# Twelve pairs of units in the second input projection as seven half-size products each

## The chip, the cores and the metric

One core of a Trainium2 chip runs one program. The metric is the device time of one execution in microseconds, the median of the runs. The engines are TensorE (PE, its weight loads PEld), VectorE (DVE), ScalarE (ACT), GpSimd (POOL) and SyncE (SP, which here only issues DMAs). Each takes its own instructions in order; semaphores tie them together.

## The reference

Two layers run one after the other on x of 1024 tokens by 1024 features, in float32. The first (attention, two recurrent mixers and a feed-forward part) is not touched. The second is:

```python
h = rmsnorm_2(x, norm_gain)
z = jnp.einsum('bsd,de->bse', h, w_in)               # 1024 -> 4864 columns
q, k, v, gate_a, u_in, v_in, gate_b, g_merge = jnp.split(z, IN_SPLITS, axis=-1)
...
attn = block_attention(q, k, v) * jax.nn.silu(gate_a)
y_a = jnp.einsum('bse,ed->bsd', attn, w_proj_attn)
u = jax.nn.gelu(u_in)
vv = layernorm(jax.nn.gelu(v_in), ln_v_gain, ln_v_bias)
vv = vv.reshape(B, S // CHUNK_2, CHUNK_2, N_GROUPS, GROUP_DIM)
v_mix = jnp.einsum('gij,bcjgd->bcigd', w_spatial, vv) + b_spatial.T[:, :, None]
gm = u * v_mix.reshape(B, S, GMLP_WIDTH) * jax.nn.silu(gate_b)
y_b = jnp.einsum('bse,ed->bsd', gm, w_proj_gmlp)
g = jax.nn.sigmoid(g_merge.reshape(B, S, N_BRANCHES, D_MODEL) + b_merge)
y = g[:, :, 0, :] * y_a + g[:, :, 1, :] * y_b
return x + jnp.einsum('bsd,de->bse', y, w_out)
```

## The kernel before, in words

Every large product is made of three: each operand is split into a high part (`h_hi`, `w_hi`, rounded to the matmul's type) and a low part (`h_lo`, `w_lo`, the rest), and hi x hi, lo x hi and hi x lo are added in PSUM. Activations are held transposed: features on the 128 partitions, tokens along the free axis, in eight row blocks. A **unit** is 128 columns of a weight matrix: for each half of 512 tokens eight row blocks by three matmuls of 128x512, 48 matmuls. Its result fills two of the four `gemm` banks. GpSimd splits a unit's weights (w_hi, then w_lo, 128x1024 each) as soon as the unit that used the same buffer two before is done.

The units of the second projection have kinds: `vi` (v_in), `ga` and `gb` (the gates), `u2` (u_in), `sga` and `sgb` (the two halves of g_merge). ScalarE evicts each with its function: gelu, silu or sigmoid.

The first block's gate and up projections already use another scheme, the item **mul**: two units are taken together, as a 2x2 block matrix of weights (column block, feature half) times one of activations (feature half, token half), by seven products of half size in place of eight (Strassen-Winograd's kind). A product has four row blocks by three matmuls, 12, in one bank. Five of the seven weights are sums of two blocks (`weight_sum`, GpSimd; `wsum`), each is rounded by ScalarE (`hi_of_quarter`) and its low part made by GpSimd (`weight_low`). Five of the activations' blocks are sums too, made once: three in own tiles (`cmb`), two in the place of blocks that nobody needs any more. After the products ScalarE copies three to `m1`, `m4` and `m3`, and VectorE adds them up in eight operations in `mul`, four of which (`final`) give a quarter of the result. The products of a pair come in the order `MUL = (0, 3, 1, 2, 4, 6, 5)`; the first takes bank 1, then 2, 3, 0, 1, 2, 3, so the fifth needs the first one's bank and its weight slot.

The function `schedule` writes one list of items, and every engine walks through it and emits its part of each item; so the list sets the order on each engine. After the attention (`a2...`) it has: `vi` 0 to 3 with their transposes (`viT`), `ga` 1, `ga` 2 with `ln` behind it, `ga` 3, `u2` 0 to 3, `gb` 0 followed by four `sp` items, `gb` 1 by four more, `gb` 2 and 3, `split4`, and then four rounds of `sga`, `sgb`, `ya`, `yb`.

- `ln` is the layer norm of vv. TensorE transposes w_spatial (`wsr` to `wsT`); VectorE copies half of wsT, sums vv, subtracts the mean; ScalarE squares (`lsq`); VectorE makes the reciprocal root and runs sixteen passes over vv (L2584 and L2586). The last signals `ln_done`.
- `sp` c is the spatial product of a chunk of 128 tokens, 16 matmuls of vv by wsT into one of four side banks, which rotate. TensorE waits for `ln_done` ahead of `sp` 0. VectorE evicts with the bias (L2612) and multiplies into uT (L2613).
- `split4` rounds aoT (gated attention) and uT to hi and lo for `ya` and `yb`, the output projections of the branches (24 matmuls a unit); these are multiplied by the sigmoid tiles and added to yT. `splity` rounds yT for the last projection, `wo2`.

Of the kernel before, what the change touches and what calls it, by code (L numbers as in the profile page):

```python
# [70 lines left out]
def weight_units():  # L71
# [48 lines left out]
    add("w_in_2", 8, 0, [(O2_V, 128)], [("v2", 0)])  # L120
    add("w_in_2", 8, 0, [(O2_GA, 128)], [("ga", 0)])
    for o, kind in ((O2_VI, "vi"), (O2_GA, "ga"), (O2_U, "u2"), (O2_GB, "gb")):
        for j in range(kind == "ga", 4):
            add("w_in_2", 8, 0, [(o + 128 * j, 128)], [(kind, j)])
    for j in range(0, 8, 2):
        for s in range(2):
            add("w_in_2", 8, 0, [(O2_M + 128 * (j + s), 128)], [("sga", j + s)])
        for s in range(2):
            add("w_in_2", 8, 0, [(O2_M + 1024 + 128 * (j + s), 128)], [("sgb", j + s)])
# [2520 lines left out]
```

## Time and profile before

| | |
|---|---|
| runs before, median (lowest to highest) | 2293.89 us (2293.43 to 2296.59) |
| profiled execution, its own time | 2298.19 us |
| its span, first to last instruction | 2296.4 us |
| mean granted TensorE clock | 0.976 |
| TensorE / VectorE / ScalarE / GpSimd busy | 92% / 53% / 38% / 39% |

The page's busy shares are means over very different stages. Times of rows are microseconds from the span's start. Matmuls overlap in the profile: each is shown with 0.39 us, but they start 0.23 us apart.

### The profile page before, as it was taken

How to read it: one execution, taken by the hardware profiler on the slowest of the kernel's cores; microseconds unless marked ns; L12 is line 12 of the kernel's file. 1: busy time of each engine (PE TensorE's matmuls, PEld its weight loads, DVE VectorE, ACT ScalarE, POOL GpSimd, SP SyncE). 2: the span in 40 equal slices, each digit the busy share in tenths (PEclk: the TensorE clock that was granted, in tenths of full speed). 3: DMA queues.
4: the chain of work that ended last, by engine and by line, in shares of the span. 5: the costliest groups of instructions: out<-in, count | busy, mean ns of one | idle time of the engine just before them, and what ended most of it. 6: DMA issues, size and time to landing. Idle time of an engine off the chain costs nothing. (4 is left out here: it accounts for less than half of the span.)

```text
span 2296.4 us, 29464 instructions
## 1 busy us (share of the span) xinstructions
PE 2122.5 (92%) x10819; PEld 1781.0 (78%) x10819; DVE 1228.5 (53%) x1811; ACT 863.4 (38%) x1562; POOL 889.4 (39%) x612
## 2 busy tenths in 40 slices
PE   6999988878998999999999968879999999999997
PEld 6788877768787788888877757768887888888886
DVE  4443503866547734444489897679995235110232
ACT  4332216555224443434444544238774122000112
POOL 1232331331335688888732642220000333333334
PEclk9999999989999999999999989999999999999999
DMA  4111310021222122222274534200001111111131
GB/s 153 41 46 46 83 55 19 19 48 36 85 71 84 43 58 68 72 70 68 78 243 140 186 101 143 93 28 1 1 2 33 47 47 39 53 46 47 54 119 74
DMA packets 181824, 157.44 MB, mean 69 GB/s; under 512 B 27588, under 2 KB 147120, under 8 KB 181552
## 3 DMA queue, kind: packets, MB, share of 16 engines
q1 hardware_dynamic: 163904, 119.05, 17.5%
q10 hardware_dynamic: 17776, 36.51, 4.3%
q8 instruction: 87, 1.43, 0.3%
q14 instruction: 57, 0.47, 0.1%
HBM read 134.03 MB, written 21.50 MB: 68 GB/s over the span
## 5 line engine op out<-in xcount | busy, mean ns | idle before, releaser
L1123 POOL TENSOR_SCALAR w_hi<-w_raw 128x1024 fp32r<-128x1024 f32 x91 | 105.9, 1163 | 940.9 <-issue 893.6
L1235 PE MATMUL gemm<-h_hi,w_hi 128*128 128x512 f32 x1072 | 423.6, 395 | 4.9 <-POOL h_lo L1152 4.9
L1237 PE MATMUL gemm<-h_hi,w_lo 128*128 128x512 f32 x1072 | 419.1, 391 | 0.0
L1236 PE MATMUL gemm<-h_lo,w_hi 128*128 128x512 f32 x1072 | 419.1, 391 | 0.0
L1235 PEld LDWEIGHTS gemm<-h_hi,w_hi 128*128 128x128 f32 x1072 | 202.6, 189 | 49.4 <-issue 8.7
L1237 PEld LDWEIGHTS gemm<-h_hi,w_lo 128*128 128x128 f32 x1072 | 202.3, 189 | 42.7
L1236 PEld LDWEIGHTS gemm<-h_lo,w_hi 128*128 128x128 f32 x1072 | 202.7, 189 | 40.8
L1126 POOL TENSOR_TENSOR w_lo<-w_raw,w_hi 128x1024 fp32r<-128x1024 f32 x91 | 229.8, 2525 | 7.6
L875 POOL TENSOR_TENSOR w_lo<-wsum,w_hi 128x512 fp32r<-128x512 f32 x122 | 165.0, 1352 | 84.2 <-ACT w_hi L1693 78.9
L1693 ACT ACTIVATE w_hi<-wsum 128x512 fp32r<-128x512 f32 x155 | 98.1, 633 | 143.2 <-PE gemm L1315 58.8
L1313 PE MATMUL gemm<-h_hi,w_hi 128*128 128x512 f32 x320 | 124.6, 389 | 0.8 <-issue 0.8
L1315 PE MATMUL gemm<-h_hi,w_lo 128*128 128x512 f32 x320 | 124.5, 389 | 0.0
L1314 PE MATMUL gemm<-h_lo,w_hi 128*128 128x512 f32 x320 | 124.5, 389 | 0.0
L2109 DVE SCALAR_TENSOR_TENSOR cacc<-cin,cols,cacc 128x1024 f32<-128x1024 f32 x42 | 66.9, 1594 | 90.0 <-ACT cacc L1641 89.0
L866 POOL TENSOR_TENSOR wsum<-w_raw 128x512 f32<-128x512 f32 x55 | 81.2, 1476 | 81.0 <-DVE w_lo L875 73.6
L875 POOL TENSOR_TENSOR w_lo<-w_raw,w_hi 128x512 fp32r<-128x512 f32 x62 | 88.3, 1424 | 44.6 <-ACT w_hi L1693 27.1
L1679 ACT ACTIVATE sig<-gemm,cols 128x1024 f32<-128x1024 f32 x16 | 18.1, 1129 | 210.0 <-PE gemm L1237 209.9
L1313 PE MATMUL gemm<-cmb,w_hi 128*128 128x512 f32 x240 | 93.4, 389 | 2.9 <-POOL w_lo L875 2.9
L2078 DVE TENSOR_TENSOR PT<-side,PT 128x512 fp32r<-128x512 f32 x128 | 88.5, 691 | 10.0 <-ACT PT L2020 6.2
L1315 PE MATMUL gemm<-cmb,w_lo 128*128 128x512 f32 x240 | 93.4, 389 | 0.0
L1314 PE MATMUL gemm<-cmb,w_hi 128*128 128x512 f32 x240 | 93.4, 389 | 0.0
L2020 ACT ACTIVATE PT<-side 128x512 fp32r<-128x512 f32 x128 | 76.5, 598 | 44.2 <-PE side L1563 39.6
(439 smaller groups left out, 4649.1 us busy)
## 6 DMA issues: line engine op xcount, KB each, us to landing
w_raw<-in_ffn_w_down SPq DMA_DIRECT2D x132, 256.0 KB, 3.1
w_raw<-in_w_in SPq DMA_DIRECT2D x60, 512.0 KB, 3.8
w_raw<-in_ffn_w_gate SPq DMA_DIRECT2D x22, 512.0 KB, 4.0
w_raw<-in_ffn_w_up SPq DMA_DIRECT2D x22, 512.0 KB, 4.3
w_raw<-in_w_out SPq DMA_DIRECT2D x16, 512.0 KB, 3.8
xin<-in_x SPq DMA_DIRECT2D x8, 512.0 KB, 6.3
x<-in_x ACTq DMA_DIRECT2D x1, 4096.0 KB, 16.0
x_spill<-x ACTq DMA_DIRECT2D x2, 2048.0 KB, 6.6
```

The costliest lines, as they stand in the source:

```text
L866: step(ops.tensor_tensor(wsum[sum_of[n]["buf"]][:], x, y, op), "w_sum" if who == "pool" else "w_sum_v")
L875: ops.tensor_tensor(quarter(wlo, slot), x, quarter(whi, slot), ALU.subtract).then_inc(w_split, 1)
L1123: gp.tensor_scalar(hi[:], raw[key % 4][:], 1.0, 0.0, ALU.mult, ALU.add).then_inc(pool_hi, 1)
L1126: gp.tensor_tensor(lo[:], raw[key % 4][:], hi[:], ALU.subtract).then_inc(w_split, 1)
L1235: mm(o, hi[:, k, m], act[0][:, k, t], start=k == 0, stop=False)
L1236: mm(o, hi[:, k, m], act[1][:, k, t], start=False, stop=False)
L1237: last = mm(o, lo[:, k, m], act[0][:, k, t], start=False, stop=k == kt - 1)
L1313: mm(o, hi[:, k, :], b[0], start=k == 0, stop=False)
L1314: mm(o, hi[:, k, :], b[1], start=False, stop=False)
L1315: last = mm(o, lo[:, k, :], b[0], start=False, stop=k == 3)
L1693: step(af(quarter(whi, slot), x, ACT.Copy), "w_quarter_hi")
L2078: ins = v.tensor_tensor(dst, b, hi, ALU.subtract)
```

## The change

Of the second projection's 32 units for gates, u_in and v_in, 24 are taken in 12 pairs through `mul`: u2 (2, 3), gb (0, 1), gb (2, 3), ga (2, 3), and the eight of sga and sgb. vi 0 to 3, ga 0 and 1 and u2 0 and 1 stay plain units.

- **c2** 0 to 2 make the three activation sums with own tiles (`cmb2`), behind vi 0, 1 and 2. The full activations are no longer there, so a sum is made twice: VectorE adds the high parts of two blocks into one of m1, m4, m3 and ca, GpSimd the low parts into `wt`, VectorE adds both, ScalarE rounds (hi), VectorE subtracts (lo). Each has four row blocks, so 12 operations on VectorE, four on GpSimd, four on ScalarE, all 128x512. **c3** 0 and 1 do the same for the two that overwrite blocks of h; they wait for the last plain unit and stand between the `sp` items.
- `sp` now only evicts, into `vm` (in vv's place); uT is multiplied by it in the pair gb (0, 1) (`mixed`), by the gates in the pair behind (`gated_by`), in quarters.
- All sigmoids are now made ahead of `ya` and `yb`. Four tiles (`quad`) hold pairs of them; five of eight are stored to DRAM (`sig_spill`, 1 MB each) by ScalarE's queue and loaded again (`sig` items) during `ya` and `yb`.
- `split4` is in two parts, inside the last merged pair; `splity` follows each `yb`; yT is four rotating tiles `yt`.

```diff
+MERGED = [("u2", 2), ("gb", 0), ("gb", 2), ("ga", 2)] + [(kind, j) for j in (6, 4, 2, 0) for kind in ("sga", "sgb")]
+SIGS = [m for m in MERGED if m[0] in ("sga", "sgb")]
+STORED = 5
+RELOADS = (("sga", 2, 3), ("sga", 4, 0), ("sgb", 4, 1), ("sga", 6, 3), ("sgb", 6, 2))
 # schedule
-    run([("vi", j) for j in range(4)], lambda kd: [(0, ("viT", kd[1]))])
+    for j in range(4):
+        run([("vi", j)], lambda kd: [(0, ("viT", kd[1]))])
+        s += [("c2", j)] * (j < 3)
     run([("ga", 1)], lambda kd: [(0, ("ln", 0))])
-    run([("ga", 2), ("ga", 3)])
-    run([("u2", j) for j in range(4)])
-    run([("gb", 0)], lambda kd: [(0, ("sp", c)) for c in range(4)])
-    run([("gb", 1)], lambda kd: [(0, ("sp", c)) for c in range(4, 8)])
-    run([("gb", 2), ("gb", 3)])
-    s.append(("split4", 0))
+    run([("u2", 0), ("u2", 1)])
+    s += [("sp", 0), ("sp", 1), ("c3", 0), ("sp", 2), ("sp", 3), ("sp", 4), ("c3", 1), ("sp", 5), ("sp", 6), ("sp", 7)]
+    for kd in MERGED:
+        for i in range(7):
+            s += [("mul", (by[kd], i))]
+            if kd == MERGED[-1]:
+                s += [("split4", 0)] * (i == 2) + [("split4", 1)] * (i == 4)
+    s.append(("sig", 0))
     for j in range(0, 8, 2):
-        run([("sga", j), ("sga", j + 1), ("sgb", j), ("sgb", j + 1)])
-        s += [("splity", k) for k in range(6 * (j == 6))]
         run([("ya", j), ("ya", j + 1)])
+        s += [("sig", 1)] * (j == 0) + [("sig", 3)] * (j == 2)
         for x in (j, j + 1):
             run([("yb", x)])
-            s += [("splity", x)] * (j == 6)
+            s += [("splity", x - 1)] * (x > 0)
+        s += [("sig", 2)] * (j == 0) + [("sig", 4)] * (j == 2)
+    s.append(("splity", 7))
 # GpSimd
+                elif kind == "c3":
+                    gemm_product(pool, unit_of["u2", 1])
+                    for k in range(4):
+                        (r1, t1), (r2, t2), op = pair_of(3 + j, k)
+                        if 4 * j + k >= 2:
+                            pool.wait_ge(N["c3_s"], 4 * j + k - 1)
+                        step(gp.tensor_tensor(wt[k % 2][:], hF[1][:, r1, t1], hF[1][:, r2, t2], op), "c3_w")
 # ScalarE, mul: before the first copy
+                    if n == first_merged:
+                        act.wait_ge(N["c2_lo"], 12)
+                        act.wait_ge(N["c3_lo"], 8)
 # VectorE
+                elif kind == "c3":
+                    gemm_product(dve, unit_of["u2", 1])
+                    for k in range(5):
+                        if k < 4:
+                            (r1, t1), (r2, t2), op = pair_of(3 + j, k)
+                            step(v.tensor_tensor(bsum[k][:], hF[0][:, r1, t1], hF[0][:, r2, t2], op))
+                            dve.wait_ge(N["c3_w"], 4 * j + k + 1)
+                            step(v.tensor_tensor(bsum[k][:], bsum[k][:], wt[k % 2][:], ALU.add), "c3_s")
+                        if k > 0:
+                            (r1, t1), _, _ = pair_of(3 + j, k - 1)
+                            dve.wait_ge(N["c3_hi"], 4 * j + k)
+                            step(v.tensor_tensor(hT[0][:, r1, t1], bsum[k - 1][:], hT[1][:, r1, t1], ALU.subtract), "c3_lo")
                 elif kind == "sp":
-                    step.frees(v.tensor_tensor(spt[:], b[:].rearrange("p (i n) -> p i n", i=4), bsp[:], ALU.add), (it, 0))
-                    step(v.tensor_tensor(uT[:, :, hslice(j)], uT[:, :, hslice(j)], spt[:], ALU.mult))
+                    step.frees(v.tensor_tensor(vm[:, j], b[:].rearrange("p (i n) -> p i n", i=4), bsp[:], ALU.add), (it, 0))
 # VectorE, mul
+            def gates(n, i):
+                x = MERGED.index(units[n]["kind"])
+                if x == 1:
+                    if i < 5:
+                        mixed(i - 1, 0)
+                        mixed(i - 1, 1)
...
```

How the order changes, in three places. First TensorE around the spatial products (`L1603` before, `L1685` after; `h` in place of `cmbs` is a plain unit's operand). Before, the first four stand behind gb0 and ahead of gb1:

```order
L1236 MATMUL gemm<-h_lo,w_hi_56 128x512
L1237 MATMUL gemm<-h_hi,w_lo_58 128x512
L1603 MATMUL side<-wsT,vv 64x128 x32
L1235 MATMUL gemm<-h_hi,w_hi_55 128x512
L1236 MATMUL gemm<-h_lo,w_hi_55 128x512
```

Now all eight (64 matmul rows) stand behind the plain unit u2 1 and ahead of the first merged product:

```order
L1313 MATMUL gemm<-h_hi,w_hi_56 128x512
L1314 MATMUL gemm<-h_lo,w_hi_56 128x512
L1315 MATMUL gemm<-h_hi,w_lo_58 128x512
L1685 MATMUL side<-wsT,vv 64x128 x64
L1395 MATMUL gemm<-cmbs_0_282,w_hi_55 128x512
L1396 MATMUL gemm<-cmbs_1_283,w_hi_55 128x512
L1397 MATMUL gemm<-cmbs_0_282,w_lo_57 128x512
```

The unit of u2 and the gates that stood ahead of them are merged and come behind.

Second VectorE, from the end of the layer norm (L2586 before, L2743 after). Before, a gate, the first two gb gates and then the evictions and multiplications of `sp`:

```order
L2584 SCALAR_TENSOR_TENSOR vv<-vv,rs,lnp 128x512
L2586 TENSOR_TENSOR vv<-vv,lnp 128x512
L2121 TENSOR_TENSOR aoT<-aoT,gaT 128x1024
L2125 TENSOR_TENSOR uT<-uT,gbt 128x1024 x2
L2612 TENSOR_TENSOR spt<-side,bsp 128x512
L2613 TENSOR_TENSOR uT<-uT,spt 128x4x128
L2612 TENSOR_TENSOR spt<-side,bsp 128x512
L2613 TENSOR_TENSOR uT<-uT,spt 128x4x128
```

After, with what each row waits for: two evictions (L2791), then c3 0 (from L2782; `m` and `ca` are the scratch, `wt` GpSimd's part):

```order
L2741 SCALAR_TENSOR_TENSOR vv<-vv,rs,lnp 128x512 [waits dve_step]
L2743 TENSOR_TENSOR vv<-vv,lnp 128x512 [waits dve_step]
L2791 TENSOR_TENSOR vv<-side,bsp 128x512 [waits side_done3,ln_done]
L2791 TENSOR_TENSOR vv<-side,bsp 128x512 [waits side_done0,side_read3]
L2782 TENSOR_TENSOR m_239<-h_hi 128x512 [waits gemm_done3,side_read0]
L2784 TENSOR_TENSOR m_239<-m_239,wt_290 128x512 [waits c3_w,dve_step]
L2782 TENSOR_TENSOR m_240<-h_hi 128x512 [waits c3_s]
L2784 TENSOR_TENSOR m_240<-m_240,wt_291 128x512 [waits c3_w,dve_step]
L2788 TENSOR_TENSOR h_hi<-m_239,h_lo 128x512 [waits c3_hi,c3_s]
L2782 TENSOR_TENSOR m_241<-h_hi 128x512 [waits c3_lo]
L2784 TENSOR_TENSOR m_241<-m_241,wt_290 128x512 [waits c3_w,dve_step]
L2788 TENSOR_TENSOR h_hi<-m_240,h_lo 128x512 [waits c3_hi,c3_s]
```

The other rows of c3 0 follow, then three evictions, and then c3 1, which looks the same.

Third ScalarE, around the norm's squares (`lsq`). Before:

```order
L1668 ACTIVATE gaT<-gemm 128x1024
L2003 ACTIVATE wsT<-side 128x512
L1626 ACTIVATE lsq,ss<-vv 128x512 x8
L1668 ACTIVATE gaT<-gemm 128x1024
L1668 ACT_TABLE_LOAD
L1668 ACTIVATE uT<-gemm 128x1024 x4
L1673 ACT_TABLE_LOAD
L1673 ACTIVATE gbt<-gemm 128x1024 x4
```

After:

```order
L1750 ACTIVATE uT<-gemm 128x1024
L1764 ACTIVATE w_hi_55<-wsum_246 128x512
L2090 ACTIVATE wsT<-side 128x512
L1708 ACTIVATE lsq,ss<-vv 128x512 x8
L1750 ACTIVATE uT<-gemm 128x1024
L1764 ACTIVATE w_hi_56<-w_raw_52 128x512
L1764 ACTIVATE w_hi_56<-wsum_245 128x512
L1764 ACTIVATE w_hi_55<-w_raw_51 128x512
L2138 ACTIVATE h_lo<-m_239 128x512
L2138 ACTIVATE h_lo<-m_240 128x512
L2138 ACTIVATE h_lo<-m_241 128x512
```

Ahead of the squares stands now a u2 unit and a first weight part of the merged products, behind them the second u2 unit, three weight parts and the roundings of c3 (`h_lo<-m`), and only behind those the copy of the first merged product.

## Rows read from the trace of the kernel before

**Rows 1.** The page: engines' busy time in us, share of the span, instructions.
```profile
span 2296.4 us, 29464 instructions
PE 2122.5 (92%) x10819; PEld 1781.0 (78%) x10819; DVE 1228.5 (53%) x1811; ACT 863.4 (38%) x1562; POOL 889.4 (39%) x612
```
**Rows 2.** Waits of TensorE, 1757 to 2296: total us, times, longest.
```profile
PE gemm L1235 <- issue: 1.6, 1, 1.6
PE side L1593 <- DVE ot L2602: 0.5, 1, 0.5
```
**Rows 3.** One stretch: us, busy time (x instructions), PEclk, DMA share, GB/s.
```profile
782.00:1085.00 303.00, 303.00 (x1339) 250.88 (x1338) 126.63 (x161) 119.99 (x193) 258.16 (x192) 1.00 0.24 66
```
**Rows 4.** Timeline of ScalarE, a u2 unit: start, us, [idle before].
```profile
1871.73 1.03 ACT L1668 ACTIVATE uT<-gemm 128x1024 f32<-128x1024 f32 x1 [9.85 <-PE gemm L1237]
```
**Rows 5.** Timeline of ScalarE, first block's pairs: first products and one w_hi.
```profile
788.48 0.60 ACT L1746 ACTIVATE m<-gemm 128x512 f32<-128x512 f32 x1 [0.79 <-PE gemm L1315]
789.70 0.63 ACT L1693 ACTIVATE w_hi<-wsum 128x512 fp32r<-128x512 f32 x1 [0.62 <-POOL wsum L866]
807.52 0.60 ACT L1746 ACTIVATE m<-gemm 128x512 f32<-128x512 f32 x1 [1.46 <-PE gemm L1315]
```
**Rows 6.** Timelines of VectorE, ScalarE and GpSimd, weight splits and layer norm.
```profile
1770.46 2.40 POOL L1126 TENSOR_TENSOR w_lo<-w_raw,w_hi 128x1024 fp32r<-128x1024 f32 x1
...
1828.42 1.22 DVE L2121 TENSOR_TENSOR aoT<-aoT,gaT 128x1024 f32<-128x1024 f32 x1 [7.52 <-ACT gaT L1668]
...
1862.96 2.77 DVE L2586 TENSOR_TENSOR vv<-vv,lnp 128x512 f32<-128x512 f32 x1
...
1828.35 0.60 ACT L2003 ACTIVATE wsT<-side 128x512 f32<-128x512 f32 x1
...
1839.15 1.05 POOL L1123 TENSOR_SCALAR w_hi<-w_raw 128x1024 fp32r<-128x1024 f32 x1 [7.25 <-issue]
...
1850.03 1.32 POOL L1123 TENSOR_SCALAR w_hi<-w_raw 128x1024 fp32r<-128x1024 f32 x1 [7.34 <-issue]
1851.44 2.71 POOL L1126 TENSOR_TENSOR w_lo<-w_raw,w_hi 128x1024 fp32r<-128x1024 f32 x1
```
**Rows 7.** The same beside and without company: VectorE, then GpSimd.
```profile
753.09 0.69 DVE L844 TENSOR_TENSOR cmb<-m,cmb 128x512 fp32r<-128x512 f32 x1
753.82 0.69 DVE L2293 TENSOR_TENSOR ca<-hfull 128x512 f32<-128x512 f32 x1
...
766.49 12.61 DVE L844 TENSOR_TENSOR h_lo<-hfull,h_hi 128x512 fp32r<-128x512 f32 x8
...
773.52 1.62 POOL L866 TENSOR_TENSOR wsum<-w_raw,w_raw 128x512 f32<-128x512 f32 x1
...
792.40 1.29 POOL L875 TENSOR_TENSOR w_lo<-wsum,w_hi 128x512 fp32r<-128x512 f32 x1
```
**Rows 8.** Timelines of ScalarE (gb0, gb1) and VectorE (one eviction).
```profile
1904.36 1.02 ACT L1673 ACTIVATE gbt<-gemm 128x1024 f32<-128x1024 f32 x1 [8.56 <-PE gemm L1237]
1919.11 1.02 ACT L1673 ACTIVATE gbt<-gemm 128x1024 f32<-128x1024 f32 x1 [13.72 <-PE gemm L1237]
...
1906.73 0.69 DVE L2612 TENSOR_TENSOR spt<-side,bsp 128x512 f32<-128x512 f32 x1
```
**Rows 9.** A long wait of TensorE and the stretches around it.
```profile
1423.55 6.69 PE L1349 MATMUL side<-diag,x_second 128*128 128x128 f32 x34 [7.93 <-DVE diag L2326]
...
1425.00:1430.00 5.00, 5.00 (x29) 5.00 (x29) 1.54 (x3) 2.06 (x3) 0.00 (x0) 0.59 0.00 0
```
**Rows 10.** Issue of a store (ScalarE's queue); DMA issues: count, KB, us to landing.
```profile
878.19 0.34 ACTq L1736 DMA_DIRECT2D f_spill<-sg  x1
...
zg<-z_spill SPq DMA_DIRECT2D x1, 1024.0 KB, 5.3
```
**Rows 11.** Timelines of VectorE and TensorE ahead of the last yb units.
```profile
2175.54 8.68 DVE L2621 TENSOR_TENSOR h_lo<-yT,h_hi 128x1024 fp32r<-128x1024 f32 x6 [41.16 <-ACT h_hi L2035]
...
2185.58 0.47 PE L1235 MATMUL gemm<-gm_hi,w_hi 128*128 128x512 f32 x1 [1.57 <-issue]
```

More of the change, by code:

```diff
@@ L119, in weight_units, with second @@
         add("w_in_2", 8, 0, [(O2_Q + 128 * j, 128)], [("q2", j)])
[L120 to L124, printed above, removed]
+    def second(kind, j):
+        o = {"v2": O2_V, "ga": O2_GA, "vi": O2_VI, "u2": O2_U, "gb": O2_GB, "sga": O2_M, "sgb": O2_M + 1024}[kind]
+        add("w_in_2", 8, 0, [(o + 128 * j, 128)], [(kind, j)])
+    for kind, j in [("v2", 0), ("ga", 0)] + [("vi", j) for j in range(4)] + [("ga", 1), ("u2", 0), ("u2", 1)]:
+        second(kind, j)
+    for kind, j in MERGED:
+        second(kind, j)
+        second(kind, j + 1)
     for j in range(0, 8, 2):
[L126 to L129, printed above, removed]
         add("w_proj_attn_2", 4, 0, [(128 * j, 256)], [("ya", j), ("ya", j + 1)])
@@ L488, in build_program @@
     f_dram = nc.dram_tensor("f_spill", [16, P, 512], F32).ap()
+    sig_dram = nc.dram_tensor("sig_spill", [STORED, P, 2 * T], F32).ap()
     x_blocks = nc.dram_tensor("x_blocks", [2, P, 1024], F32).ap()
@@ L818, in mul_weight, with mul_operand @@
                     (a21, a11, ALU.subtract), (a12, a22, ALU.subtract)][MUL[j[1]]]
-        def mul_operand(i, k):
+        def mul_operand(i, k, second=False):
             p, lo, hi = MUL[i], slice(0, 512), slice(512, 1024)
+            if second and p in (0, 3, 2):
+                return [cmb2[(0, 3, 2).index(p)][x][:, k, :] for x in range(2)]
+            if second and p in (5, 6):
+                r, t = {5: (k, hi), 6: (4 + k, lo)}[p]
+                return [hT[1][:, r, t], hT[0][:, r, t]]
             if p in (0, 3, 2):
@@ L1728, in final @@
                     count = 4 * pairs_before(n) + (2, 4, 5, 6).index(i) + 1
-                    if kind == "gate":
+                    if units[n]["kind"] in MERGED:
+                        j = units[n]["kind"][1]
+                        x = merged_place(n, i)
+                        gemm_consumed(act, (n, i))
+                        if kind in ("sga", "sgb"):
+                            c = 88 + 8 * (kind == "sgb") + j + m
+                            step(af(x, x, ACT.Sigmoid, bias=cols[:, c:c + 1]), "quad_ready")
+                            if i == 6 and stored_at(kind, j) is not None:
+                                y = stored_at(kind, j)
+                                act.dma_start(sig_dram[y], quads[quad_of[kind, j]][:].rearrange("p m n -> p (m n)")).then_inc(sig_out[y], 16)
+                        else:
+                            step(af(x, x, ACT.Gelu_apprx_tanh if kind == "u2" else ACT.Silu), "quad_ready")
+                    elif kind == "gate":
                         gemm_consumed(act, (n, i))
@@ L2152, in final @@
                     p = units[n]["kind"][1] // 2
+                    if units[n]["kind"] in MERGED:
+                        if i == 2 and units[n]["kind"] in SIGS:
+                            y = SIGS.index(units[n]["kind"])
+                            if y >= 3:
+                                dve.wait_ge(sig_out[y - 3], 16)
+                        add(merged_place(n, i), x, ALU.add, True)
+                        return
                     if kind == "gate":
@@ L2165, in mul @@
                     return
+                if units[n]["kind"] in MERGED[1:]:
+                    gates(n, i)
                 gemm_product(dve, j)
```

205 lines of the change are left out of this document (149 added, 56 removed).

## The prediction

> **What bounds the kernel now.** First the page: TensorE is busy 92% of the span, VectorE 53%, GpSimd 39%, ScalarE 38% [rows 1]. Shares alone don't tell what a stage costs, so the next view is the list of waits of TensorE, cut to the stretch from 1757 us, where the second input projection begins, to the end. It holds two waits, 2.1 us together in 539 us [rows 2]. Everything in this part is set by the number of products, and whatever removes one there ends the program sooner, as long as no new wait appears. The table by stretch is the third view: TensorE is busy the whole of 782 to 1085 [rows 3], where the first block's gate and up projections already run as seven half-size products, at the full clock. So the scheme that the change extends is known to run there without a wait, and its pace can be read.
>
> **What is saved.** One plain unit (two token halves, eight row blocks, three matmuls each, 48 in all) takes 10.88 us: ScalarE, which takes each as it ends, waits 9.85 us for a u2 unit and works 1.03 on it [rows 4]. One merged pair (seven products of 12 matmuls, 84 instead of 96) takes 19.04 us: the first product of two pairs is copied at 788.48 and 807.52 [rows 5]. Before: 24 x 10.88 = 261.1 us. After: 12 x 19.04 = 228.5 us. The saving is 32.6 us if nothing waits. Everything else that TensorE does is kept in number.
>
> **The wait for the layer norm.** The eight spatial products read vv after its layer norm, and TensorE waits for ln_done ahead of the first. Before, twelve units stand between the attention and them (four vi, ga1 to ga3, four u2, gb0); now only seven (vi0 to vi3, ga1, u2_0, u2_1). The seventh plain unit ended at 1839.1 (GpSimd's split at 1839.15 waited for it [rows 6]), and the same seven units with the same transposes stand there now. The norm isn't done then. Before, its chain on VectorE ran from the copy of wsT, right behind a gate multiply that ended at 1829.64, over the sum, the mean's subtraction, the squares on ScalarE and sixteen passes over vv to 1862.96 + 2.77 = 1865.7 [rows 6]; nobody waited for it, since u2 and gb0 lay in front. The change leaves every instruction of this chain. It takes away that multiply (1828.42, 1.22 us), and TensorE's transposes of wsr are ready at 1828.35 (ScalarE reads their first half then), so the chain can start 1.3 us sooner and ends at 1864.4. Its sixteen passes began at about 1848.2, behind the squares, and took 17.5 us; at 0.73 to 0.8 each, 12.2 us would do; they ran beside two splits of GpSimd (the first 1.32 + 2.71 = 4.0 us, the second like it: 8.1 us). Now six quarter operations of GpSimd, 1.37 us each with their gap [rows 7], fall there: 8.2 us, so I keep 17.5. TensorE waits 1864.4 - 1839.1 = **25.3 us**. Bounds: without GpSimd's company 5.3 us less; up to 1.5 us more, should the first weight operations of the merged part meet the subtraction.
>
> **The sums of c3 between the spatial products.** Count from the end of the norm. Four spatial products cost 3.87 us: gb0 and gb1 are taken at 1904.36 and 1919.11, 14.75 apart, with one unit of 10.88 between [rows 8]; so 0.97 each. VectorE evicts the first two (0.69 each [rows 8]) and is free for c3 0 at +2.8; I add 1.0 for the clock (below): +3.8. c3 is twice twelve VectorE operations on 128x512, chained with four of GpSimd and four of ScalarE. Alone such an operation takes 0.73 us with its gap (753.09 to 753.82); beside GpSimd's it takes 12.61 / 8 = 1.58, and GpSimd's own goes from 1.29 to 1.62, a pace of about 1.68 for one of each [rows 7]. So each GpSimd operation that falls there adds 0.95 us to VectorE's 0.73. I count four in c3 0 (two of its own, two of c3 1) and three in c3 1: 8.7 + 3.8 = 12.5 and 8.7 + 2.9 = 11.6 us. There are four side banks: the seventh spatial product needs the third evicted, which on VectorE stands behind c3 0. So c3 0 ends at +16.3, three evictions +18.5, c3 1 +30.1. On ScalarE the copy of the first merged product waits for all of c3, because m1 is also c3's scratch; then it copies (0.60), makes the fifth product's w_hi (0.63), and GpSimd its w_lo (1.29 [rows 5, 7]): +32.8 with gaps. The fifth product needs both the bank and the slot. TensorE's work up to there is 8 x 0.97 + 4 x 2.72 = 18.6 us. Lost: **14.2 us**. Bounds: c3 free of company 17.5 us in place of 24.1, 6.6 less; every operation of it beside GpSimd 1.65 x 24 = 39.6, 15.5 more.
>
> The rows of [rows 7] say that one VectorE operation with two SBUF inputs goes with one of GpSimd. The Trainium skill (SBUF — State Buffer, "SBUF: two separate sides") says it harder: the shared port pair is an exclusive lock, held for the whole instruction, by either a VectorE operation with two SBUF inputs or a GpSimd one. By the trace a pair costs 1.68 us, by the rule 0.73 + 1.37 = 2.10, so c3 would last 27.2 instead of 24.1 and the result be 3.1 us later; the trace agrees in kind, and I keep its number.
>
> **The clock.** After a wait of 7.93 us TensorE was granted a mean of 0.59 of its full 2.4 GHz in a stretch of 5 us, so mostly the lower level of 1.2, and loses 2 us of it [rows 9]. Two such restarts come: at the first spatial product, and at the seventh after some 9 us of waiting. The first delays the evictions (1.0 us, in the sum), the second lies inside the time up to the fifth product, which is set by VectorE. Bounds 0 and 3.
>
> **The rest.** c2 (three times the same twelve operations) lies beside vi0 to ga1. GpSimd can't begin it before it has split vi2's weights, to 1772.9 [rows 6]; a part then takes 12 x 0.73 + 2 x 0.95 + 2.4 beside the next split (3.45 us of GpSimd) = 13.1 us, and 0.7 for the copy behind it: the parts end at 1786, 1800 and 1814. ScalarE takes vi1, vi2 and vi3 only behind c2's copies, so vi3 at 1812.5 + 1.0 in place of 1803.7; u2_0 needs its bank at 1816.4. No wait, with 3 us to spare: 0, up to 3. In the merged pairs GpSimd has 12 operations of 1.37, 16.4 of 19.04 us; VectorE has 8, and in the gb pair also 8 with vm and two gates: about 20 us of work in one pair, with 3 us of slack carried in. I take 1.0 for it (0 to 4). The issue of a store of 256 KB cost ScalarE's queue 0.34 us; of 1 MB, 1.4 us if it grows with the size, once a pair, where ScalarE was busy only 120 of 303 us in the first block's stretch [rows 3]. A 1 MB load landed in 5.3 us [rows 10], and the first reloaded tile is used four units of 24 matmuls, 21.8 us, after its issue: hidden. If this cover were gone, it would be 5.3 us once. The wait of 1.57 us at 2185.58 goes: it came from six splits of yT (8.68 us) that held up two evictions on VectorE [rows 11], and they are now spread: -1.6.
>
> **Sum.** -32.6 + 25.3 + 14.2 + 1.0 - 1.6 = **+6.3 us**. The profiled execution took 2298.19 us, 1.8 more than its span of 2296.4; on its footing 2304.5. The median of the runs is 2293.89, 4.3 below; the change goes on it: **2300.2 us**.
>
> **Rivals.**
> 1. Two waits of the same size as the saving, inside the measurement. A measurement of this kernel tells 0.2%, 4.6 us, from no change. With c3 free of most of GpSimd (-3 to -6), or the sixteen passes so (-3 to -5), the sum is 0 to +3: 2294 to 2297. For it: on 753 to 755 VectorE did run such operations at 0.73. Against: GpSimd's operations are part of the same chain. Chance 0.20.
> 2. Faster: both chains at their free ends and no loss of clock, -7.6: 2286. In the far case that TensorE doesn't meet the end of the norm at all, it keeps 32.6 + 1.6 less c3's 14: 2274. Against both: the chain of the norm is unchanged and was measured. Chance 0.09.
> 3. VectorE falls behind for good. The place is the gb pair: its mixing and gate operations have two SBUF inputs and GpSimd works 16.4 of 19 us, so all at 1.58: 10 x 1.58 + 8 x 0.73 = 21.6 us, on top of c3's leftovers; it decides if the pair begins with VectorE more than 3 us late. With c3 at 30 us instead of 24 and c2 delaying u2_0 by 2: +6.3 + 6 + 4 + 2 = 2312. Chance 0.16.
> 4. The products are not saved at all: excluded by the order of instructions, where 12 matmuls of a pair are gone.
>
> The forecast itself, +4.6 to about +13, has 0.55. Slower by over 0.2% is it and rival 3, 0.71; within, 0.20; faster, 0.09. The range 2291 to 2310 leaves out rival 2, the slow half of rival 3 and little else.
>
> **What would show it.** Right: TensorE's waits from 1757 us show one of about 25 us ahead of the first spatial product, released by VectorE's last pass over vv; one of about 8 to 9 ahead of the seventh; one of a few us at the fifth product; the later pairs 19.04 us apart; a clock of 0.5 in two stretches. Wrong: the norm ending before 1855, c3 0 under 9 us, pairs over 19.5 us apart, or waits in ya and yb for reloaded tiles.

## The result, and the profile after

The median is 2316.84 us (2314.13 to 2318.15), the kernel before on the same chip 2293.94; the ratio is 1.0089, with an interval of 1.0076 to 1.0103 (the two medians divided give 1.0100, inside it). So the change costs 17 to 24 us, about three times the +6.3 of the prediction, and 2316.84 lies above its range of 2291 to 2310. In the profiled executions it is 19.3 us (2317.47 against 2298.19).

On the page TensorE's busy time is shorter and the span longer, so the loss is waiting.

```profile
span 2315.6 us, 30174 instructions
PE 2096.1 (91%) x10675; PEld 1757.6 (76%) x10675; DVE 1367.9 (59%) x1973; ACT 957.7 (41%) x1726; POOL 1030.6 (45%) x728
```

TensorE's waits of the changed kernel from 1757 us (total, times, longest), where [rows 2] had 2.1 us:

```profile
PE side L1685 <- DVE vv L2743: 25.3, 1, 25.3
PE side L1685 <- DVE vv L2791: 10.5, 1, 10.5
PE side L1405 <- ACT vist L1736: 5.9, 2, 3.8
PE gemm L1313 <- DVE quad L2292: 2.8, 1, 2.8
PE gemm L1395 <- POOL w_lo L937: 1.7, 2, 1.5
```

The first is the wait for the norm (forecast 25.3), the second that of the seventh spatial product (forecast 8 to 9), the last is in part that of the fifth merged product (1.5; forecast a few us). The third and the fourth were not forecast.

The unchanged part ahead of this stage ends at another time in each profiled execution (1753.4 to 1758.0 us over the eleven kernels of this study), so stages are measured from vi0's first matmul. First of before, then of after, that matmul and the first one of the last output unit (start, duration); of after also that of u2_1, the last plain unit (1834.52), and those behind the long waits:

```profile
1758.02 0.47 PE L1235 MATMUL gemm<-h_hi,w_hi 128*128 128x512 f32 x1
...
2272.72 0.39 PE L1292 MATMUL side<-w_hi,h_hi 128*128 128x512 f32 x1
```

```profile
1756.92 0.47 PE L1313 MATMUL gemm<-h_hi,w_hi 128*128 128x512 f32 x1
...
1834.52 0.47 PE L1313 MATMUL gemm<-h_hi,w_hi 128*128 128x512 f32 x1
...
1871.00 1.33 PE L1685 MATMUL side<-wsT,vv 128*64 128x128 f32 x10 [25.31 <-DVE vv L2743]
...
2126.54 0.47 PE L1313 MATMUL gemm<-at_hi,w_hi 128*128 128x512 f32 x1 [2.83 <-DVE quad L2292]
...
2291.88 0.39 PE L1370 MATMUL side<-w_hi,h_hi 128*128 128x512 f32 x1
```

That is 514.70 us before and 534.96 after, +20.3.

**Where c2 holds TensorE.** ScalarE in the changed kernel, the evictions of vi1, vi2 and vi3 into the tiles that TensorE transposes:

```profile
1787.32 1.03 ACT L1736 ACTIVATE vist<-gemm 128x1024 f32<-128x1024 f32 x1
1803.46 1.02 ACT L1736 ACTIVATE vist<-gemm 128x1024 f32<-128x1024 f32 x1
1819.30 1.02 ACT L1736 ACTIVATE vist<-gemm 128x1024 f32<-128x1024 f32 x1
```

They are 16.1 and 15.8 us apart; a unit with its transposes takes 11.8. Each stands behind a part of c2. In the kernel before, TensorE began the transposes of vi3 without a wait at 57.2 us of the stage (1815.26 - 1758.02):

```profile
1815.26 1.03 PE L1323 MATMUL side<-con,st 128*128 128x128 f32 x8
```

Here vi3's tile is evicted only from 62.4 on. VectorE in the second part of c2, with the copy of transposed blocks behind it (L2538), and GpSimd's w_lo in the same time:

```profile
1789.75 0.69 DVE L2771 TENSOR_TENSOR m<-h_hi 128x512 f32<-128x512 f32 x1
...
1791.93 1.66 DVE L2773 TENSOR_TENSOR m<-m,wt 128x512 f32<-128x512 f32 x1
...
1797.51 2.77 DVE L2776 TENSOR_TENSOR cmbs<-m,cmbs 128x512 fp32r<-128x512 f32 x1
...
1805.13 0.69 DVE L2538 COPY vv<-side 128x512 f32<-128x512 f32 x1
```

```profile
1797.02 2.71 POOL L1188 TENSOR_TENSOR w_lo<-w_raw,w_hi 128x1024 fp32r<-128x1024 f32 x1
```

The same kind of operation takes 0.69, 1.66 or 2.77 us. VectorE has no idle time in these 15.4 us (1789.75 to 1805.13).

**The end of the last pair.** VectorE, ScalarE and GpSimd ahead of the first `ya` unit:

```profile
2115.62 8.49 DVE L2796 TENSOR_TENSOR at_lo<-aoT,at_hi 128x1024 fp32r<-128x1024 f32 x4 [1.28 <-ACT at_hi L2122]
...
2125.59 0.69 DVE L2292 TENSOR_TENSOR quad<-m,gemm 128x512 f32<-128x512 f32 x1
```

```profile
2118.84 0.60 ACT L1834 ACTIVATE m<-gemm 128x512 f32<-128x512 f32 x1
```

```profile
2119.77 3.26 POOL L1188 TENSOR_TENSOR w_lo<-w_raw,w_hi 128x1024 fp32r<-128x1024 f32 x1
```

Four subtractions of split4 (8.49 us) stand ahead of the additions that free the banks; the last of three additions ends at 2126.3, and TensorE has waited 2.83 us for it.

**The clock** (the stretch, its length, busy times, and third from the end the granted clock as a share of the full 2.4 GHz, ahead of DMA):

```profile
1820.00:1825.00 5.00, 4.62 (x18) 4.08 (x19) 4.86 (x5) 3.83 (x5) 2.34 (x2) 0.66 0.36 105
...
1865.00:1870.00 5.00, 0.00 (x0) 0.00 (x0) 4.79 (x7) 0.00 (x0) 0.00 (x0) 0.50 0.00 0
1870.00:1875.00 5.00, 4.00 (x40) 4.00 (x42) 1.80 (x4) 0.00 (x0) 0.00 (x0) 0.53 0.01 3
...
1885.00:1890.00 5.00, 1.25 (x12) 1.25 (x14) 4.76 (x6) 0.63 (x1) 1.70 (x1) 0.50 0.00 0
...
2126.00:2131.00 5.00, 4.46 (x13) 3.54 (x14) 4.90 (x4) 0.73 (x1) 1.47 (x1) 0.66 0.32 106
```

0.50 is the level of 1.2 GHz. It was granted in both long waits and still behind them. Two more stretches have a mean of 0.66, so in part that level: behind the 3.84 us wait for vi3's tile, and behind the 2.83 us.

### The profile page after: what moved, and what is told of

It is laid out like the page before. It is cut to its first block and busy times, and to the rows that moved or that the text cites. A ratio compares the mean times of both kernels' runs of the same rounds, so it can differ in the third digit from the quotient of the medians.

```text
span 2315.6 us, 30174 instructions
## 1 busy us (share of the span) xinstructions
PE 2096.1 (91%) x10675; PEld 1757.6 (76%) x10675; DVE 1367.9 (59%) x1973; ACT 957.7 (41%) x1726; POOL 1030.6 (45%) x728
## 5 line engine op out<-in xcount | busy, mean ns | idle before, releaser
L937 POOL TENSOR_TENSOR w_lo<-wsum,w_hi 128x512 fp32r<-128x512 f32 x182 | 246.4, 1354 | 126.0 <-ACT w_hi L1764 117.3
L1313 PE MATMUL gemm<-h_hi,w_hi 128*128 128x512 f32 x688 | 274.4, 399 | 5.0 <-POOL h_lo L1230 5.0
L1315 PE MATMUL gemm<-h_hi,w_lo 128*128 128x512 f32 x688 | 270.1, 393 | 0.0
L1314 PE MATMUL gemm<-h_lo,w_hi 128*128 128x512 f32 x688 | 269.9, 392 | 0.0
L1188 POOL TENSOR_TENSOR w_lo<-w_raw,w_hi 128x1024 fp32r<-128x1024 f32 x67 | 168.8, 2519 | 5.6
L1395 PE MATMUL gemm<-h_hi,w_hi 128*128 128x512 f32 x416 | 162.0, 389 | 2.2 <-POOL w_lo L937 1.5
L1396 PE MATMUL gemm<-h_lo,w_hi 128*128 128x512 f32 x416 | 161.9, 389 | 0.0
L1397 PE MATMUL gemm<-h_hi,w_lo 128*128 128x512 f32 x416 | 161.8, 389 | 0.0
L1313 PEld LDWEIGHTS gemm<-h_hi,w_hi 128*128 128x128 f32 x688 | 130.7, 190 | 34.2 <-issue 8.4
L1315 PEld LDWEIGHTS gemm<-h_hi,w_lo 128*128 128x128 f32 x688 | 130.4, 190 | 28.0
L1314 PEld LDWEIGHTS gemm<-h_lo,w_hi 128*128 128x128 f32 x688 | 130.8, 190 | 25.8
L928 POOL TENSOR_TENSOR wsum<-w_raw,w_raw 128x512 f32<-128x512 f32 x96 | 129.9, 1353 | 7.5
L1395 PE MATMUL gemm<-cmb,w_hi 128*128 128x512 f32 x240 | 93.4, 389 | 2.9 <-POOL w_lo L937 2.9
```

The costliest lines, as they stand in the source:

```text
L928: step(ops.tensor_tensor(wsum[sum_of[n]["buf"]][:], x, y, op), "w_sum" if who == "pool" else "w_sum_v")
L937: ops.tensor_tensor(quarter(wlo, slot), x, quarter(whi, slot), ALU.subtract).then_inc(w_split, 1)
L1188: gp.tensor_tensor(lo[:], raw[key % 4][:], hi[:], ALU.subtract).then_inc(w_split, 1)
L1313: mm(o, hi[:, k, m], act[0][:, k, t], start=k == 0, stop=False)
L1314: mm(o, hi[:, k, m], act[1][:, k, t], start=False, stop=False)
L1315: last = mm(o, lo[:, k, m], act[0][:, k, t], start=False, stop=k == kt - 1)
```

## The experiments

The second column has medians; the last three are us from vi0's first matmul ("the stage") in the profiled execution, one of each kernel.

| kernel | median us | ratio to before | norm's end | first ya | last output unit |
|---|---|---|---|---|---|
| before | 2293.9 | 1 | 107.7 | (219.1) | 438.5 + 76.2 |
| changed | 2316.8 | 1.0089 | 114.0 | 369.6 | 458.8 + 76.2 |
| e1 c2 later | 2312.4 | 1.0074 (1.0061 to 1.0088) | 110.0 | 365.7 | 454.8 |
| e2 split4 spread | 2310.8 | 1.0070 (1.0056 to 1.0084) | 114.1 | 367.3 | 455.8 |
| e3 ga plain | 2298.0 | 1.0016 (1.0007 to 1.0025) | 111.8 | 352.5 | 441.7 |
| e4 c2, c3 on VectorE | 2306.3 | 1.0050 (1.0037 to 1.0062) | 105.3 | 360.2 | 449.4 |
| e5 c2 on VectorE | 2309.9 | 1.0059 (1.0046 to 1.0071) | 106.2 | 361.8 | 452.6 |
| e6 no c3 | 2303.4 | 1.0035 (1.0022 to 1.0049) | 113.1 | 355.1 | 444.4 |
| b2 combined | 2283.6 | 0.9950 (0.9937 to 0.9962) | 103.8 | 339.1 | 427.6 |
| b3 order | 2283.9 | 0.9954 (0.9940 to 0.9967) | 103.8 | 339.6 | 428.1 |
| b4 c3 on TensorE | 2273.9 | 0.9910 (0.9897 to 0.9924) | 103.8 | 329.4 | 417.9 |

In before the first ya unit stands ahead of most gates, so its 219.1 compares with no other. The last column is the start of the first wo2 matmul; from there to the last unit it is 76.2 us in both kernels, and it is what "stage" means in the comparisons below.

### e1: c2's parts one unit later

```diff
-        s += [("c2", j)] * (j < 3)
+        s += {0: [("c2", 0)], 2: [("c2", 1)], 3: [("c2", 2)]}.get(j, [])
```

> The second of the three parts of c2 stands one unit later (behind vi2 instead of vi1) and the third behind vi3, so ScalarE evicts vi2 and vi3 ahead of the rounding copies that held them; nothing else moves. Theory A (c2's part takes 16.1 us against a unit's 11.8, and on ScalarE it stands ahead of the evictions for which TensorE's transposes wait): the waits of 2.03 and 3.84 us and the slow stretches behind them go, the layer norm starts about 6.6 us sooner and ends near 1864.5, and the whole is 6.5 to 8 us shorter, 2309 to 2310.5. Theory B (VectorE's work as a whole is the bound from 1773 to 1902, and the order on ScalarE only passes it on): the two waits go, but the norm ends at 1871 as now and the total stays within 1 us of 2316.8.

Measured: 4.4 us less in the median, 4.0 in the stage. The two transposes no longer wait; but c2's last part now stands ahead of ga1's eviction, and u2_1 waits for its bank:

```profile
1825.95 0.47 PE L1313 MATMUL gemm<-h_hi,w_hi 128*128 128x512 f32 x1 [1.92 <-ACT gaT L1750]
1864.02 1.34 PE L1685 MATMUL side<-wsT,vv 128*64 128x128 f32 x10 [26.90 <-DVE vv L2743]
```

Theory A had the place and the sign, not the size: the norm ends 4.0 us sooner, not 6.6, and the whole is 4.4 shorter, not 6.5 to 8. Theory B (nothing) is out.

### e2: split4 spread

```diff
-                s += [("split4", 0)] * (i == 2) + [("split4", 1)] * (i == 4)
+                s += {1: [("split4", (0, 0))], 2: [("split4", (0, 1))], 3: [("split4", (0, 2))], 4: [("split4", (0, 3))],
+                      5: [("split4", (1, 0)), ("split4", (1, 1))]}.get(i, [])
+    s += [("sig", 0), ("split4", (1, 2)), ("split4", (1, 3))]
```

> The two parts of split4, four operations of ScalarE and four of VectorE each, are spread over the products of the last merged pair and its end, one or two at a time. Theory A (four roundings and four subtractions in one piece hold the copy of the fourth product and the additions that free the banks): the 2.83 us wait ahead of the first ya unit and the stretch at the lower clock behind it go, 4 to 5.1 us less, about 2312. Theory B (the wait comes from the last finals and would be there in any order): no change, 2316 to 2317.

Measured: 6.0 us less in the median, 3.0 in the stage. Of the 2.83 us two small waits are left:

```profile
PE gemm L1313 <- DVE quad L2292: 0.6, 1, 0.6
...
PE gemm L1313 <- DVE at_lo L2796: 0.4, 1, 0.4
```

The wait was the block of split4 (Theory A), and 3 us of the 5.1 lost there come back, less than the 4 to 5.1 expected. The median's 6.0 holds more than the stage shows; the intervals of the two ratios overlap (1.0076 to 1.0103 and 1.0056 to 1.0084), so the size rests on the stage, that is on one execution of each kernel.

### e3: ga (2, 3) as plain units ahead of the spatial products

```diff
-MERGED = [("u2", 2), ("gb", 0), ("gb", 2), ("ga", 2)] + ...
+MERGED = [("u2", 2), ("gb", 0), ("gb", 2)] + ...
...
-    run([("u2", 0), ("u2", 1)])
+    run([("ga", 2), ("ga", 3), ("u2", 0), ("u2", 1)])
```

> The pair ga (2, 3) is taken back to two plain units, which stand between ga1 and u2_0, so 21.8 us of products more stand ahead of the spatial products, for 19.04 less behind. Theory A (TensorE lacks work ahead of the end of a norm whose time is set by VectorE alone): the wait of 25.3 us falls to 3 to 6, the cost is 2.7 us, so 16 to 20 us less, 2297 to 2301. Theory B (the norm's passes share with GpSimd, whose weight splits of the plain units now fall beside them, and end 6 to 8 us later): 9 to 12 us less, 2305 to 2308.

Measured: 18.9 us less, 17.1 in the stage: Theory A's amount. The wait for the norm is 1.18 us (3 to 6 were expected). But the wait of the seventh spatial product grew from 10.49 us:

```profile
1869.75 5.46 PE L1685 MATMUL side<-wsT,vv 128*64 128x128 f32 x96 [1.18 <-DVE vv L2747]
...
1891.51 3.68 PE L1685 MATMUL side<-wsT,vv 128*64 128x128 f32 x32 [16.30 <-DVE vv L2795]
```

VectorE shows why: c3 0's second operation waits for GpSimd, which first has the weight operations that the last plain unit set free.

```profile
1877.92 1.78 DVE L2788 TENSOR_TENSOR m<-m,wt 128x512 f32<-128x512 f32 x1 [3.91 <-POOL wt L1225]
```

### e4 and e5: the sums without GpSimd

```diff
 # VectorE, c2 and c3 (e5: c2 alone); GpSimd's part goes
...
-                            dve.wait_ge(N["c2_w"], 4 * j + k + 1)
-                            step(v.tensor_tensor(bsum[k][:], bsum[k][:], wt[k % 2][:], ALU.add), "c2_s")
+                            step(v.tensor_tensor(bsum[k][:], bsum[k][:], hF[1][:, r1, t1], ALU.add))
+                            step(v.tensor_tensor(bsum[k][:], bsum[k][:], hF[1][:, r2, t2], op), "c2_s")
```

> In c2 and c3 VectorE adds the low parts itself, in two additions in place, where GpSimd made a sum of them and VectorE added that: 20 operations of 128x512 more on VectorE, 20 less on GpSimd. Theory A (an operation of GpSimd with two inputs costs a VectorE operation beside it 0.95 us, more than the 0.73 that VectorE takes for it alone): a part of c2 takes 15 us instead of 16.1 and c3 0 about 11.8 instead of 12.7, 2 to 5 us less in all, 2312 to 2315. Theory B (GpSimd's part is free help): 20 x 0.73 = 14.6 us more work on the engine that TensorE waits for, 2326 to 2331.

> Only c2 is computed without GpSimd; c3 stays as in the changed kernel. It tells apart where the 9 to 10 us that the same edit to both saved come from. Theory A (c2 with GpSimd takes 16.1 us a part and is the cause of the 7.8 us that TensorE loses before u2_0): the waits of 2.03 and 3.84 us go, the norm ends near 105.5 us after the stage's start instead of 114.0, and 7 to 9 us of the gain are here, 2307 to 2310. Theory B (the gain lay in c3's chain, which c2 only delayed): 0 to 3 us, 2313 to 2317.

Measured: e4 is 10.5 us faster than the changed kernel (9.4 in the stage), with 20 operations more on VectorE, at least twice what Theory A gave; Theory B's sign is wrong. c3 0 of e4, where GpSimd is idle, is a row of operations of 0.69:

```profile
1865.08 0.69 DVE L2782 TENSOR_TENSOR m<-h_hi 128x512 f32<-128x512 f32 x1
1865.80 0.69 DVE L2783 TENSOR_TENSOR m<-m,h_lo 128x512 f32<-128x512 f32 x1
...
1876.04 0.69 DVE L2788 TENSOR_TENSOR h_hi<-ca,h_lo 128x512 fp32r<-128x512 f32 x1
```

Sixteen operations from 1865.08 to 1876.73 are 11.7 us; with GpSimd twelve took 12.5 (1875.52 to 1888.0). This is the clean comparison of the two ways: 0.8 us for a part of c3, as Theory A had it.

e5 is 6.9 us faster than the changed kernel (6.2 in the stage), and puts the larger gain in its place: the norm's end moves from 114.0 to 106.2 and the first ya unit by 7.8 us with c2 alone, Theory A. But this is not the price of sharing alone. c2 now also begins at once, where in the changed kernel VectorE waited 13.29 us for GpSimd's first sum, queued behind vi2's weights.

```profile
1773.23 1.81 DVE L2773 TENSOR_TENSOR m<-m,wt 128x512 f32<-128x512 f32 x1 [13.29 <-POOL wt L1218]
```

The evictions of vi1, vi2 and vi3 in e5:

```profile
1778.69 1.03 ACT L1736 ACTIVATE vist<-gemm 128x1024 f32<-128x1024 f32 x1 [0.92 <-PE gemm L1315]
...
1795.84 1.03 ACT L1736 ACTIVATE vist<-gemm 128x1024 f32<-128x1024 f32 x1
...
1811.11 1.03 ACT L1736 ACTIVATE vist<-gemm 128x1024 f32<-128x1024 f32 x1
```

The first part is done before vi1 is, so vi1 waits for nothing; behind it the evictions are 17.2 and 15.3 us apart, no closer in sum than with GpSimd (16.1 and 15.8), since two weight splits fall into the second part and VectorE has sixteen operations in each. So what freed the transposes in e4 and e5 is for the most part the start of the chain; no run changes the sharing in c2 without its start.

In e5 1.6 of the 7.8 us are lost again in the ya units: in the table 369.6 - 361.8 = 7.8, but 458.8 - 452.6 = 6.2. There TensorE waited twice (2.80 and 1.82 us), and the granted clock was 0.66 over 5 us (2126 to 2131) behind the second wait, where the changed kernel's slow stretch stands behind its only one; why it fell there is open.

### e6: c3 left out

```diff
-                elif kind == "c3":            # on ScalarE, VectorE and GpSimd
-                        act.wait_ge(N["c3_lo"], 8)
```

> The changed kernel with c3 left out: the two sums of activations that overwrite blocks of h are not made, and the last two products of each pair are taken with the plain blocks that lie there (so the two products' factors are other numbers; the number of matmuls is the same). It measures the term of c3 by itself. Theory A (c3 alone makes TensorE wait between the spatial products and the fifth product): the waits of 10.49 and 1.47 us and the clock lost behind them go, 13 to 16 us less, 2301 to 2304; the wait of 25.3 us for the norm and the two early ones stay. Theory B (GpSimd's and ScalarE's weight operations for the first pair, which now come first, need as long): 5 us less or under, 2311 and above.

Measured: 13.4 us less in the median, 14.4 in the stage (Theory A). Both waits are gone. The price of c3 was +14.2 in the prediction, and here it is 14.4; 0.9 of it lies ahead of the norm's end (113.1 in place of 114.0), where two of c3's GpSimd sums no longer stand beside the norm's passes.

### b2: e2, e3 and e4 together

> Three edits together: ga (2, 3) as two plain units ahead of the spatial products, split4 spread over the last merged pair, and c2 and c3 without GpSimd. Theory A (the three losses are separate and come off one by one): from the stage of 458.8 us in the changed kernel 7.8 for c2, 19 for the plain units with GpSimd no longer late for c3, 0.8 in c3 itself and 3 for split4, so 427 to 430 us against 438.5 in the kernel before; in all 2283 to 2287. Theory B (VectorE's work is the bound, so what one edit frees the next wait takes): not below 2294.

Measured: 2283.59 us, the stage 427.6; Theory A's sum. This is 0.5% faster than the kernel before (the interval of the ratio excludes 1). The largest wait left is the seventh spatial product's:

```profile
PE side L1685 <- DVE vv L2795: 13.4, 1, 13.4
```

### b3: another order, and scratch of its own

```diff
+    m = [("mul", (by[MERGED[0]], i)) for i in range(7)]
+    s += [("sp", c) for c in range(4)] + [("c3", 0), m[0], m[1], ("sp", 4), ("sp", 5), m[2], ("c3", 1), ("sp", 6), ("sp", 7)] + m[3:]
```

> The same as the combined kernel, and c3 has scratch of its own, so the copies of the first two products of the first merged pair need not wait for it; the order is four sp, c3 0, two products, two sp, a product, c3 1, two sp, and the other products. Theory A (TensorE's wait inside the spatial products is set by the evictions queued behind c3 0, the one at the fifth product by c3's scratch): the wait ahead of the seventh sp goes, one of 7 to 9 us stays at the last product of the pair, which needs c3 1; 5 to 7 us less than the combined kernel, 2276 to 2281. Theory B (VectorE's work from the end of the norm to the end of c3 1 is the same, so the end of the pair is too): within 2 us of the combined kernel.

Measured: 2283.88 us, the stage 428.1: no gain, Theory B. The 13.4 us are gone from where they were, and stand at the last products of the pair (three waits on c3's `h_hi`) and at the first of the next:

```profile
PE gemm L1397 <- DVE h_hi L2795: 6.8, 3, 4.3
PE gemm L1397 <- POOL w_lo L939: 1.7, 2, 1.4
PE gemm L1397 <- DVE uT L2299: 1.6, 1, 1.6
```

This order doesn't help: the sum of VectorE's work is what is waited for.

### b4: c3's sums by TensorE

```diff
 # on b2; TensorE, four matmuls by the identity in a side bank per block
...
+                    for k in range(4):
+                        b = bank((it, k))
+                        x, y, _ = pair_of(3 + j, k)
+                        ops = [(i, r, t) for r, t in (x, y) for i in (0, 1)]
+                        for q, (i, r, t) in enumerate(ops):
+                            last = mm(b[:], identr[:], hT[i][:, r, t], start=q == 0, stop=q == 3)
+                        done(last, (it, k))
...
 # ScalarE and VectorE
...
+                        step(af(hT[1][:, r1, t1], b[:], ACT.Copy), "c3_hi")
...
+                        step.frees(v.tensor_tensor(hT[0][:, r1, t1], b[:], hT[1][:, r1, t1], ALU.subtract), (it, k))
```

> The combined kernel, with c3's sums made by TensorE: four matmuls of 128x512 by the identity add the high and low parts of two blocks in a side bank, ScalarE rounds and VectorE subtracts from it, so VectorE has 8 operations in c3 in place of 32 and TensorE 32 matmuls more (7.3 us at 0.227); all eight spatial products stand ahead of c3, and the first copy waits for it no more. Theory A (VectorE's work between the norm's end and c3's end is what TensorE waits for): the 13.4 us wait at the seventh sp goes and the first merged product starts 14 to 16 us after the first sp, not 22.5, with no wait at the fifth; 8 to 12 us less than the combined kernel, 2272 to 2276. Theory B (TensorE's own 7.3 us and eight evictions of side banks, each through ScalarE and VectorE, cost as much): within 3 us of the combined kernel.

Measured: 2273.86 us, 9.7 less than b2 (9.7 in the stage too; Theory A), 0.9% faster than the kernel before and 1.9% than the changed one. From the first sp to the first merged product it is 14.5 us, of which the 32 matmuls of c3 take 7.4:

```profile
1857.24 7.21 PE L1696 MATMUL side<-wsT,vv 128*64 128x128 f32 x128 [1.12 <-DVE vv L2759]
1864.38 0.50 PE L1686 MATMUL side<-h_hi,identr 128*128 128x512 f32 x1
...
1871.77 0.39 PE L1396 MATMUL gemm<-cmbs,w_hi 128*128 128x512 f32 x1
```

VectorE in it has one operation of 0.69 each 0.91 us, the time of four matmuls:

```profile
1866.36 0.69 DVE L2798 TENSOR_TENSOR h_hi<-side,h_lo 128x512 fp32r<-128x512 f32 x1 [1.10 <-ACT h_lo L2154]
1867.27 0.69 DVE L2798 TENSOR_TENSOR h_hi<-side,h_lo 128x512 fp32r<-128x512 f32 x1 [0.22 <-ACT h_lo L2154]
```

## Why the prediction was wrong

The sign and the two large waits were right; the size was not. Two steps failed: c2 was taken to cost nothing and cost 7.8 us, and the split4 inside the last pair was not in the sum and cost 5.1. With 1.0 more at c3 they make 13.9 of the 14.0 us between forecast and stage. Step by step, in the stage:

| step | forecast | measured |
|---|---|---|
| products saved | -32.6 | -32.6 |
| c2 beside vi0 to ga1 | 0 (up to 3) | +7.8 |
| wait for the norm | +25.3 | +25.3 |
| spatial products with c3 | +14.2 | +15.2 |
| the gb pair on VectorE | +1.0 | +1.0 |
| split4 inside the last pair | not priced | +5.1 |
| old wait at the yb units | -1.6 | -1.8 |
| sum | +6.3 | +20.0 of 20.3 |

**Products.** ScalarE copies the first product of two later pairs at these times, 19.04 us apart as in [rows 5]:

```profile
1955.19 0.60 ACT L1832 ACTIVATE m<-gemm 128x512 f32<-128x512 f32 x1 [0.79 <-PE gemm L1397]
...
1974.23 0.60 ACT L1832 ACTIVATE m<-gemm 128x512 f32<-128x512 f32 x1 [0.79 <-PE gemm L1397]
```

**c2: the step that failed.** "No wait, with 3 us to spare." That ScalarE takes vi1 to vi3 only behind c2's copies was in the prediction; the pace of c2 was wrong, and so was the place where TensorE needs the result. The 3 us were counted up to u2_0's bank (1816.4), but the transposes of vi3 need the evicted tile at 1815.26, so 1.8 us were to spare behind the forecast 1813.5. It counted 2 x 0.95 + 2.4 for GpSimd in a part; the second part shows all four of GpSimd's sums beside an operation of VectorE (0.98, 0.97, 0.98 and 0.88 us more) and 2.8 for the weight split: 8.8 + 3.8 + 2.8 = 15.4, and 16.1 with the copy, where 13.8 stood. Three parts in a chain made the evictions 16 us apart against units of 11.8. vi3's came at 62.4 us of the stage where the forecast had 54.5 (1812.5 - 1758.0); 1.4 us of this is a later start (VectorE's first addition of a GpSimd sum at 16.3 instead of 14.9), the rest is the pace. So the slack was used up by the second part, and TensorE waited 2.03 and 3.84 us at the transposes. With the slower clock behind the second wait (the unit u2_0 took 11.73 instead of 10.98, the transposes 1.62 instead of 0.79; behind the first the clock stayed at 1.00) u2_1 began at 77.6 us of the stage; in the kernel before, the unit in its place began at 69.8: +7.8. (The expectation of e5 says u2_0; that one began 7.1 us late.) e5 takes GpSimd out of c2, and just these 7.8 us go. That proves c2 with GpSimd's sums as the cause; that the pace and not the wait for GpSimd's first sum is what the forecast lacked follows from its times, since it had that wait too (to 1772.9), and not from a run.

**The norm: right, but not for the times given.** TensorE was ready at 1845.7 and the norm ended at 1870.9. In the stage that is 88.8 and 114.0, against 81.1 and 106.4 in the forecast: both are 7.6 to 7.7 late, for the same reason, and the difference stayed. Whoever checks only the wait would call the whole step right. The lateness is counted once, as c2's. Luck is in it too: the sixteen passes took 15.9 us (1855.03 to 1870.94), not the 17.5 kept for them, but GpSimd's first operations fell ahead of the passes and stretched two small operations of the norm from 0.17 to 1.22 and 1.12, so that the part ahead took 1.7 more than before and the sum came out.

**c3: right within 1 us.** From the first spatial product to the fifth merged one it is 1904.77 - 1871.00 = 33.8 us, with 18.6 us of TensorE's work: 15.2. e6 takes c3 out and gains 14.4. The two parts took 12.5 and 11.7 us, forecast 12.5 and 11.6. The last operation of c3 1 on VectorE, and ScalarE's copy of the first merged product that waited for it:

```profile
1901.15 0.69 DVE L2788 TENSOR_TENSOR h_hi<-ca,h_lo 128x512 fp32r<-128x512 f32 x1
```

```profile
1902.04 0.60 ACT L1832 ACTIVATE m<-gemm 128x512 f32<-128x512 f32 x1 [0.99 <-DVE h_hi L2788]
```

**split4: missed.** The prediction priced reloads and stores in the merged pairs (0, as measured: no wait on them) and not the split in the last one. It could have been priced from [rows 11]: six such subtractions took 8.68 us, so four are 5.8 alone, and beside two weight splits more; a product leaves VectorE 2.7 us. It cost 3.0 us ahead of the first ya unit (the last three products took 11.15 instead of 8.16) and 2.1 in the first two ya units (48 matmuls: 13.02 instead of 10.88). In the changed kernel those 2.1 are the low clock; in e1 the clock was 1.00 there, and TensorE waited 1.72 us for the next bank at the same place, and the two units took 13.0 us as well. That the additions on VectorE, queued behind split4, would set this end at either clock is a reading of the two traces; e2 brings back 3.0 of the 5.1 us.

**The rest of the difference.** The medians differ by 22.9, the profiled executions by 19.3 and the stage by 20.3; all lie in the interval of the ratio, 17 to 24 us. The execution of before that was profiled lay 4.3 us above its median, and entered the stage at 1758.0, the latest of all eleven, in a stretch that the change doesn't touch. No run tells more of the 2 to 3 us between these figures, nor whether they are more than noise.

**The rivals.** Rival 3 (VectorE falls behind for good, 2312) had the engine right and the place wrong: not the gb pair, where the loss was 1.0 us, but c2 ahead of it. Of its terms "c2 delaying u2_0 by 2" was the one that came, with 7.1 us at u2_0 and 7.8 at the next unit.

**The lock.** The rule of the Trainium skill that was weighed (SBUF — State Buffer, "SBUF: two separate sides") would, worked out by pairs, have made c3 some 3 us longer than the price from the rows; c3's parts took 24.1 us in sum, so the rows' price was the right one. What the rule says of a single pair shows in c2: VectorE's 2.77 us operation began 0.49 us behind a GpSimd one of 2.71 and ended 0.55 after it, and most beside a sum of 1.73 took 1.66. The trace agrees that the one behind waits for the whole of the other, and with the weight split this waiting makes 6.6 of the 15.4 us of c2's second part. The price by pairs that the prediction took from [rows 7] held in c3 because it counted all GpSimd operations there, and failed in c2 because it didn't.

## What to carry to other kernels

A saving on the busiest engine is paid by whatever makes its operands: here 60 additional operations of VectorE, put where TensorE had its cover. Price such a chain by the sum of all that both engines with shared operands do in it, and compare its pace with that of the units it is threaded through, not only its end with a deadline. Ask first where the waiting engine needs the result (here transposes, one step ahead of the bank that was looked at). A helper engine that takes a few of a chain's operations can make it longer than without (c3 0: 12.5 us with, 11.7 without), and makes it start when the helper is free; and where the waiting engine is TensorE itself, sums of tiles by the identity in PSUM take the work back to the engine that is idle (c3: 24 of VectorE's 32 operations in b2 for 7.4 us of matmuls in b4).
